# Two transformer blocks with fp32 products: a residual stream turned from features on partitions to tokens on partitions, and half of its products turned with it

## What is computed

```python
# first block
u = rmsnorm(h, g_mix_pre);  proj = u @ w_in            # 2048 -> 10240, then two attentions
mixed = sigmoid(ga) * (oa @ w_br_moba) + sigmoid(gb) * (ob @ w_br_diff)
h = h + rmsnorm(mixed @ w_out, g_mix_post)
ff = square(relu(rmsnorm(h, g_mlp_pre) @ w_up)) @ w_down      # 2048 -> 8192 -> 2048
h = h + rmsnorm(ff, g_mlp_post)
gate = sigmoid(rmsnorm(h, g_ple_pre) @ w_ple_gate)
h = h + rmsnorm((p @ w_ple_proj) * gate, g_ple_post)
# second block
z = rms_norm(x, mix_norm_g) @ w_in;  ...               # mLSTM and forgetting attention
x = x + concat(ha, hb) @ w_out
x = x + (gelu(conv(a)) * g) @ w_down                   # 2048 -> 2 x 5632 -> 2048
x = x + sigmoid(rms_norm(x, ple_norm_g) @ w_ple_gate) * (p @ w_ple_proj)
```

## Time and profile before

| what | value |
|---|---|
| time, median of 3 runs | 2920.16 us (2914.24 to 2925.27) |
| profiled execution: its own time | 2925.14 us |
| its span, first to last instruction | 2923.3 us |
| mean granted clock of TensorE | 0.987 |
| PE busy / weight loads busy | 2832.4 us (97%) / 2451.9 us (84%) |
| DVE / ACT / POOL busy | 1952.9 us (67%) / 1425.3 us (49%) / 180.5 us (6%) |
| matmuls | 15969, of them 2 x 7680 of the large products |
| DMA | 510.29 MB, 175 GB/s; weight transfers of 1024 KB land in 5.2 to 5.7 us |

### The profile page before, as it was taken

The page is one execution under the profiler, slowest core; times in us unless marked ns, Lnnn a source line. Parts: engine busy times, 40 slices in busy tenths (PEclk is TensorE's granted clock), DMA queues, the critical chain, the costliest instruction groups (busy, mean ns, idle before and its releaser), DMA issues.

```text
span 2923.3 us, 43834 instructions
## 1 busy us (share of the span) xinstructions
PE 2832.4 (97%) x15969; PEld 2451.9 (84%) x15969; DVE 1952.9 (67%) x2287; ACT 1425.3 (49%) x1757; POOL 180.5 (6%) x136
## 2 busy tenths in 40 slices
PE   7999999998999999999887999999999999999998
PEld 6888888886888888888776888778888888888877
DVE  6676766667656656566688566766777567667885
ACT  5555554444444444444454545554544444444564
POOL 2000000011000000001212000002100000000210
PEclk9999999999999999999999999999999999999999
DMA  6555546564655556555544355445565555656553
GB/s 216 173 172 171 174 162 192 182 190 126 189 185 183 191 179 194 186 184 185 163 139 122 116 184 161 153 150 187 176 195 190 189 182 191 195 179 201 165 180 130
DMA packets 499727, 510.29 MB, mean 175 GB/s; under 512 B 8586, under 2 KB 496288, under 8 KB 499648
## 3 DMA queue, kind: packets, MB, share of 16 engines
q1 hardware_dynamic: 498576, 508.39, 54.6%
q0 software_dynamic: 1072, 0.83, 0.2%
HBM read 507.09 MB, written 2.10 MB: 174 GB/s over the span
## 4 chain that ended last, share of the span: by engine, by line
PE 90%; DVE 5%; ACT 2%; issue 2%; DMA 0%; POOL 0%; DVEq 0%; SPq 0%; ACTq 0%
PE ps L1620 57%; PE ps L1621 29%; DVE split L981 2%; DVE E L1465 1%; ACT split L539 1%; PE pw L1720 1%; DMA raw<-in_w_in 0%; DVE G L1046 0%; PE pw L1656 0%; ACT X L563 0%; POOL G L431 0%; PE pw L1721 0%; PE pw L1715 0%; DVE X L1012 0%; DVE h L1037 0%
## 5 line engine op out<-in xcount | busy, mean ns | idle before, releaser
L1620 PE MATMUL ps<-X,split 128*128 128x512 f32 x7168 | 2539.0, 399 | 45.9 <-issue 32.0
L1621 PE MATMUL ps<-X,split 128*128 128x256 f32 x7168 | 2011.7, 281 | 0.0
L1620 PEld LDWEIGHTS ps<-X,split 128*128 128x128 f32 x7168 | 1353.6, 189 | 376.1 <-issue 38.3
L981 DVE TENSOR_TENSOR split<-raw,split 128x1024 fp32r<-128x1024 f32 x968 | 1199.0, 1261 | 528.6 <-ACT split L539 521.4
L1621 PEld LDWEIGHTS ps<-X,split 128*128 128x128 f32 x7168 | 1359.1, 190 | 0.8
L539 ACT ACTIVATE split<-raw 128x1024 fp32r<-128x1024 f32 x968 | 1008.6, 1055 | 689.6 <-PE ps L1621 687.0
L545 ACT ACTIVATE cross<-ps 128x512 f32<-128x512 f32 x252 | 150.4, 597 | 411.1 <-PE ps L1621 411.0
L1620 PE MATMUL ps<-split,X 128*128 128x512 f32 x512 | 185.4, 405 | 0.0
L1621 PE MATMUL ps<-split,X 128*128 128x256 f32 x512 | 144.7, 283 | 0.0
L994 DVE TENSOR_TENSOR t<-ps,cross 128x512 f32<-128x512 f32 x90 | 62.2, 691 | 110.4 <-ACT cross L545 110.4
L1620 PEld LDWEIGHTS ps<-split,X 128*128 128x128 f32 x512 | 97.3, 190 | 25.0 <-issue 2.0
(11 more groups left out here) (245 smaller groups left out, 1096.5 us busy)
## 6 DMA issues: line engine op xcount, KB each, us to landing
raw<-in_w_up SPq DMA_DIRECT2D x152, 1024.0 KB, 5.7
raw<-in_w_in SPq DMA_DIRECT2D x136, 1024.0 KB, 5.2
raw<-in_w_down SPq DMA_DIRECT2D x96, 1024.0 KB, 5.4
raw<-in_w_out SPq DMA_DIRECT2D x32, 1024.0 KB, 5.3
raw<-in_w_ple_gate SPq DMA_DIRECT2D x32, 1024.0 KB, 5.4
raw<-in_w_down SPq DMA_DIRECT2D x16, 768.0 KB, 4.5
raw<-in_w_br_moba SPq DMA_DIRECT2D x8, 1024.0 KB, 5.4
raw<-in_w_br_diff SPq DMA_DIRECT2D x8, 1024.0 KB, 5.4
```

The lines of the kernel that those rows point to most:

```text
L981: TT(split[:, k % RING, :, 1, :], raw[:, (k // 2) % RING, HALF * (k % 2):HALF * (k % 2) + HALF, :], split[:, k % RING, :, 0, :], ALU.subtr ...
L1620: MM(ps[:, bank, :], stay_hi, move, start=start, stop=False, skip_group_check=True)
L1621: ins = MM(ps[:, bank, 0:TOK], stay_lo, move[:, 0, :], start=False, stop=stop, skip_group_check=True)
```

## The change

Four things change together.

1. `h` becomes [128, 2, 2048]: tokens on partitions, two token tiles, features along the row. The input lands in it directly and the output is stored from it directly, so L2005 and L776 go, and the input's copy L578.
2. The products whose result is added to `h`, or gated for it (out1, ffn1 down, proj1, gate1, out2, ffn2 and ffn2b down, proj2, gate2), get the form "wide" (`wide_tile`): 128 tokens' activation is stationary and 512 weight columns move, three times (hi by hi, hi by lo, lo by hi) into one region of a bank. No cross half is left, so ACT's copy of it and DVE's add go in these phases; a unit is now 512 features by 256 tokens and lasts 8 halves of 2 tiles. Transfers bring 512 rows by 512 columns.
3. In the form "features", which stays for the other products, the two 512-column matmuls of a tile now come first and the two 256-column ones behind them (before, they alternated).
4. The norms: ACT squares rows with an accumulator (`square`, two of 128x512 for a quarter of the features), DVE sums 4 numbers (`norm_sum`), root and inverse are taken of 128x2 values, and DVE adds `G` times the norm's column to `h` by 2 instructions of 128x512 (`add_normed`). The gains of the post norms are multiplied in when a unit is evacuated, from rows that POOL's transfers bring. Then PE turns each quarter of `h` by 8 transposes (`turn`, L1801), and ACT and DVE make the next operand from PSUM (`gained_hi`, `gained_lo`), in steps of 2 tiles. Where a product needs the norm as a row, PE makes it from a diagonal (`norm_row`). POOL makes no squares any more.

Also, proj1 moves from behind ffn1 to behind out1; the first wide half needs 2 feature tiles of its operand and not 4; and the loops over units of out1, gate1, out2, gate2 and the last downs are written out.

```diff
 PHASES = [
-    ("moba", 4, 8, 4), ("diff", 4, 8, 4), ("branch", 4, 8, 6), ("out1", 4, 4, 2),
-    ("ffn1", 4, 32, 16), ("proj1", 1, 2, 8), ("gate1", 4, 4, 2),
...
+    ("moba", 4, 8, 4, 0), ("diff", 4, 8, 4, 0), ("branch", 4, 8, 6, 0), ("out1", 2, 8, 2, 2), ("proj1", 1, 2, 4, 4),
+    ("ffn1", 4, 32, 12, 4), ("gate1", 2, 8, 2, 2),
...
-    h = sb("h", [P, KT, TOK])
+    h = sb("h", [P, 2, DM])
...
+    wide1, wide2 = ("wide", X1, 0, 8 * (2,)), ("wide", X2, 0, 8 * (2,))
+    OUT1 = GATE = plan([wide1, wide1])
+    OUT2 = DOWN = plan([wide2, wide2])
...
+        def wide(at, g, w, col0, row0=0, rows=2048):
+            for q in range(rows // 512):
+                load(at, g + q, w[bass.ds(row0 + q * 512, 512), bass.ds(col0, WIDE)])
...
+        def square(k, c, tokens):
+            for q in range(2):
+                A(junk[:, :], tokens(q), ACT.Square, accum_out=norm_sq[:, k, q, c:c + 1]).then_inc(squares, 1)
...
-            for k in range(4):
-                kt = 4 * c + k
-                ins = A(X1[:, bass.ds(kt, 1), 0, :], h[:, bass.ds(kt, 1), :], ACT.Copy, scale=vec(gain, kt))
-            ins.then_inc(x1_hi, 1)
+            for pair in range(2):
+                act.wait_ge(x_turned, 8 * norm_of(e) + 2 * c + pair + 1)
+                for k in range(2):
+                    kt = 4 * c + 2 * pair + k
+                    ins = A(X1[:, kt, 0, :], pw[:, 2 * (c % 2) + pair, k * TOK:k * TOK + TOK], ACT.Copy, scale=vec(gain, kt))
+                ins.then_inc(x1_hi, 1)
...
+        def add_normed(k, c, src):
+            for q in range(2):
+                ins = STT(h[:, q, columns(c)], src(q), norm_col[:, k, q:q + 1], h[:, q, columns(c)], ALU.mult, ALU.add)
+            ins.then_inc(h_ready, 1)
...
                 for j in range(2):
-                    bank, js = 2 * s + j, slice(j * P, j * P + P)
...
-                    MM(ps[:, bank, :], stay_hi, move, start=start, stop=False, skip_group_check=True)
-                    ins = MM(ps[:, bank, 0:TOK], stay_lo, move[:, 0, :], start=False, stop=stop, skip_group_check=True)
+                    MM(ps[:, 2 * s + j, :], stay[:, 0, j * P:j * P + P], move, start=start, stop=False, skip_group_check=True)
+                for j in range(2):
+                    ins = MM(ps[:, 2 * s + j, 0:TOK], stay[:, 1, j * P:j * P + P], move[:, 0, :], start=False, stop=stop, skip_group_check=True)
...
+        def wide_tile(s, x, w, start, stop):
+            for q in range(2):
+                dst = ps[:, 2 * s + q, :].rearrange("p (a c) -> p a c", a=2)
+                x_hi, x_lo = (x[:, part, q * P:q * P + P] for part in range(2))
+                MM(dst, x_hi, w[:, :, 0, :], start=start, stop=False, skip_group_check=True)
+                MM(dst, x_hi, w[:, :, 1, :], start=False, stop=False, skip_group_check=True)
+                ins = MM(dst, x_lo, w[:, :, 0, :], start=False, stop=stop, skip_group_check=True)
...
+        def turn(e, c):
+            if c >= 2:
+                pe.wait_ge(x1_ready, 8 * e + 2 * c - 2)
+            for pair in range(2):
+                for k in range(2):
+                    kt = 4 * c + 2 * pair + k
+                    for q in range(2):
+                        ins = T(pw[:, 2 * (c % 2) + pair, k * TOK + q * P:k * TOK + q * P + P], h[:, q, kt * P:kt * P + P], ident)
+                ins.then_inc(x_turned, 1)
```

More of the change, by code:

```diff
@@ L1274, in embed, with out1, after @@
             TT(operand[:, :, 1, :], pw[:, 2, :].rearrange("p (a t) -> p a t", a=2), operand[:, :, 0, :], ALU.subtract).then_inc(p_ready, 1)
+        def out1(i):
+            s = At("out1", i, 8, 2)
+            def after(m):
+                if i == 0 and m == 2:
+                    embed(0, X2[:, 12:14])
+                if m % 8 == 7:
+                    n = 2 * i + m // 8
+                    row = gain_row(n)
+                    if n == 3:
+                        norm_sum(1)
+                    else:
+                        dve.wait_ge(squares, 8 + 2 * n + 2)
+                    TT(G_tok[:, :, columns(n)], wide_sums(s, m, m // 8), row, ALU.mult).then_inc(evac_done, 1)
+            each_half(s, OUT1, after)
+        out1(0)
+        out1(1)
+        norm_inverse(1)
+        dve.wait_ge(evac_done, U0["out1"] + 4)
+        s = At("proj1")
+        add_normed(1, 0, of_G(0))
+        add_normed(1, 1, of_G(1))
+        lo(s, 0)
+        add_normed(1, 2, of_G(2))
+        gained_lo(2, 0, "g_mlp_pre")
+        lo(s, 1)
+        add_normed(1, 3, of_G(3))
+        lo(s, 2)
+        gained_lo(2, 1, "g_mlp_pre")
+        lo(s, 3)
+        gained_lo(2, 2, "g_mlp_pre")
         def ffn1(b):
@@ L1528, in _, with add_h, out2, after @@
-        out2 = add_h("out2", TILES_OUT2, TWO, operand=(5, "ffn_norm_g_2"))
+        def add_h(at, m, u, n):
+            cs = columns(n)
+            dve.wait_ge(evac_done, at.unit(u))
+            TT(h[:, :, cs], h[:, :, cs], wide_sums(at, m, u), ALU.add).then_inc(evac_done, 1)
+        def out2(i):
+            s = At("out2", i, 8, 2)
+            def after(m):
+                if i == 0 and m == 2:
+                    finish_fox(1)
+                if m % 8 == 4 and (i or m > 7):
+                    gained_lo(5, 2 * i + m // 8 - 1, "ffn_norm_g_2")
+                if m % 8 == 7:
+                    add_h(s, m, m // 8, 2 * i + m // 8)
+            each_half(s, OUT2, after)
@@ L1805, in embed, with out1, before, proj_unit @@
             ins.then_inc(p_turned, 1)
+        def out1(i):
+            s = At("out1", i, 8, 2)
+            def before(m):
+                if i == 0 and m == 2:
+                    embed(0)
+            each_half(s, OUT1, x1_is(1), before)
+        out1(0)
+        out1(1)
+        def proj_unit(at, u, op, tile):
+            g = u // 2
+            unit_start(at, u)
+            if u % 2 == 0:
+                pe.wait_ge(lo_done, at.halves(2 * g) + 2)
+            first = blocks(at, 2 * g, u, "wide", op, u % 2, (tile,), True, False)
+            last = blocks(at, 2 * g + 1, u, "wide", op, u % 2, (tile + 1,), False, True)
+            if u % 2 == 0:
+                last.then_inc(pair_used, 1)
+            else:
+                first.then_inc(half_used, 1)
+                last.then_inc(half_used, 1)
@@ new lines, in _, with start_up, hidden @@
+        out2(0)
+        out2(1)
+        def ffn2(name, b, pairs, k0):
+            outer = dict(outer_turn=b * 12, outer_units=b * 20, outer_cross=b * 16) if name == "ffn2" else {}
+            first = name == "ffn2" and isinstance(b, int) and b == 0
+            def start_up(m):
+                if m == 1:
+                    pe.wait_ge(evac_done, U0["out2"] + 4)
+                    turn(5, 3)
+                if m == 4:
+                    norm_row(3, 0)
+            def hidden(m, u, upto):
```

987 lines of the change are left out of this document (520 added, 467 removed).

## The result

| | before | changed |
|---|---|---|
| median, same chip | 2922.7 us (2914.2 to 2938.5) | 2836.9 us (2834.6 to 2837.7) |
| ratio | | 0.9709, 95% interval 0.9681 to 0.9737 |
| profiled execution, and its span | 2925.1 us, 2923.3 us | 2836.1 us, 2834.3 us |

The kernel is faster by 85.8 us in the medians and by 89.0 us between the two profiled spans. The forecast was a gain of 41.5. The time fell in the predicted range, but about half of the gain has a cause to which the forecast gave nothing.

A forecast was written before the change was run, and what follows sets the result against it. PE, busy 97% of the span, was taken as the bound. Seams gain 42.1 us, extra transposes lose 4.6, the start gains 4: 41.5 in all, so 2883.6 us for a profile and 2879 for the median; range 2828 to 2908.

The forecast's parts named there:

- the pace goes by columns: Dense products: a matmul costs only its columns, so 1.5 wide matmuls cost what a 512 plus 256 pair costs; gain 0.
- the new order: Features form, 512, 512, 256, 256: same columns and loads as the alternating order, so costed at 0.
- rival 1: Dense products: the overhead is per matmul, a wide one takes 0.229 us, 22 us more gained, 2857; chance 0.15.
- the two paces: Pairs took 0.354 us in ffn1, 0.3475 in ffn2; which one a phase falls into may move 25 us either way.
- load rule: Skill's rule: a weight load takes its columns divided by 1.2 GHz, so wide matmuls would hide loads; rejected from the trace.
- The seams: Excess over dense work between phases and at the tail: 88.2 us before, 46.1 after, a gain of 42.1.
- 4.6 lost to transposes: Out2, ffn2 and ffn2b: added transposes and a norm row, less one `sum_acc`, cost 2.1 plus 2.5 us.
- the cover: Out1 to ffn1: two units of proj1, 5.6 us, stand ahead of the first transpose and hide the norm's 5.3 us chain.
- The start: First window, 51 us: the input's copy on ACT and POOL's summing go; gain 4 us.
- Rival 2: Dense products: wide matmuls run at full pace, 0.215 us each, 80 us more gained, 2799; chance 0.06.
- rival 3: Seams stay long: PE waits 1.9 us for each of four quarters at three seams, 23 us lost, 2902; chance 0.08.
- rival 4: Wide matmuls read two runs 2 KB apart and slow down; at 0.249 us each plus 63 us, 2942; chance 0.11.

The follow-up runs named there:

- Run 3: The changed kernel with each 512-column matmul of the wide form issued as two of 256, same columns and stationary blocks: 2887.4 us, a single run.
- Run 2: The changed kernel with the features products back in the old order 512, 256, 512, 256: 2848.5 us, against the changed kernel's 2836.9.
- run 1: The kernel before with only the new order, both 512-column matmuls ahead of the two 256-column ones: 2906.7 us against 2918.0, ratio 0.9967.
- run 5: The changed kernel with the operands of the wide form read as bfloat16, same number and columns of matmuls: 2827.9 us, a single run.
- Run 6: The changed kernel with proj1's products cut to one matmul per bank and tile, 7.3 us of PE work taken out: 2834.4 us, 2.5 less.
- run 7: The changed kernel with one more 128x256 reciprocal on VectorE in each of the three norms that add to the residual stream: 2840.4 us, 3.6 more.
- run 10: The control: the changed kernel itself, unchanged, measured again on another chip: 2836.9 us, ratio 0.9713 to before.

## Why the prediction was right and where it was wrong

- **The direction and the range held, the size didn't.** 41.5 us were forecast and 85.8 measured. The term that failed is in the part on the wide matmul: "the pace goes by columns ... this edit gives 0", and the next one, the new order "I cost it at 0". That the range held is partly luck: for the forecast alone the prediction gave 2850 to 2908, and 2836.9 lies in the part below, which it kept for its first rival. Its own sign, "I am wrong if the time moves inside the dense stretches, and not at the seams", came half true: the time moved in both.
- **The wide edit.** In place of 2816 pairs at 0.351 (988 us) there are 4224 matmuls at 0.2268 (958): 30 us, not 0. Run 3 shows the mechanism, cost per matmul: at 346.7 ns, columns and fixed cost alone, the pairs would have been 976 us, so 18 of the 30 come from fewer matmuls. The other 12 are what the old pairs took beyond that, which belongs to their order. The cost per matmul is rival 1, given 0.15; it had 0.229 for a wide matmul and 22 us.
- **The order.** 4864 pairs at 0.351 became 2432 quads at 0.697: 12 us, not 0. Run 2, with the same pairs, measures 11.7, and run 1, with 7680, 11.4 (2 to 17). The prediction saw the two paces, took them for a lottery of the stage and put 25 us to either side (counted on 7680 pairs; only 4864 keep the form, which is 16). Only the old order has the two paces; what picks between them under it is not shown.
- **Why the reading misled.** I fitted a + b per column to the start distances inside a mixed stream: 0.237 and 0.117, a ratio of two. In a pure stream they are 0.2268 and 0.1203. In the mixed one the 512-column step reads 7 ns too long and the 256-column step 3 ns too short, and just this makes them look proportional. Only the sum of a repeating group can be trusted there, and one sum can't give two unknowns. The trace of before did hold a warning: at 1.2 GHz a pair took 0.64 us, exactly its 768 columns, and at 2.4 GHz 0.347 at best, not 0.320. Something beyond the columns costs 27 ns a pair there, as rival 1 said; whether it goes by matmul or by column only a second width shows.
- **Weight loads.** The rejection of the Trainium skill's load rule (TensorE: Matmul & The Clock Gate, "LDWEIGHTS (loading the stationary operand)") as the limit holds: beside the earlier trace rows, run 5 halved the loads to 96 ns and moved the pace by 1.4 ns. The loads' mean stayed at 188 ns in the changed kernel.
- **The seams** of the table gained 43.1 us, forecast 42.1. With the start's 2.4 that leaves 0.5 of the 46, where the prediction had 4.6 lost to transposes in out2, ffn2 and ffn2b; this loss does not show in the remainder, and I did not trace why. The head of the seam to gate1 was 9.48 (forecast 9.3), the tail 6.6 (6.5), proj2 1.4 (2.0). out1 to ffn1 was 9.8 instead of 7.8; of this 2.3 are the wait for the norm's row, which I had at 0.4 in all. Run 6 supports the cover, and run 7 the chain and that the cover has no slack.
- **The start.** 4 us were forecast; the first 51 us have 28.5 of excess before and 26.1 now, so 2.4 came. A new wait of 1.5 us for the norm's row stands in this stretch (2.7 in run 10).
- **Rival 2** (0.215) is refuted by 0.2268, **rival 3** (seams stay long, 2902) by the table above, **rival 4** (the operand in two runs) by run 3.

## What to carry to other kernels

Price a dense matmul stream as columns plus a fixed cost per matmul, and get the two numbers from streams of one width each, never from single distances in a mixed stream. The same group at both clocks tells whether there is a cost beyond the columns, not what it goes by. Fewer, wider matmuls for the same columns then pay by a sum that can be written down, and where widths must mix, try the order: equal widths next to each other were 11 to 12 us faster here. In a seam ask which engine's chain ends last before spending on another: 1.75 us more on VectorE cost 1.6 in each seam, while a clock kept at double speed through two seams gave 0.8 in all.

## What the runs showed that I had not expected

- The fixed cost is 13.3 ns per product matmul at 2.4 GHz and is not to be seen at 1.2 GHz: there a wide matmul starts 0.42 to 0.43 us after the one before it (behind the seam from ffn1 to gate1), and 512 / 1.2 GHz is 426.7 ns.
- The same four matmuls in the order 512, 256, 512, 256 take 0.693 or 0.707 us, and 0.697 in the order 512, 512, 256, 256 in all the long dense stretches (ffn1, ffn2); in attention, among small products, it is 0.702 and more. The faster of the old paces is thus a little better than the new one, and I have no explanation for what picks the slower.
- While GpSimd summed on 128x1024 early in the kernel before, VectorE's split of the same size took about twice its length. GpSimd's and VectorE's rows there:

```profile
27.90 1.22 DVE L981 TENSOR_TENSOR split<-raw,split 128x1024 fp32r<-128x1024 f32 x1
...
29.20 9.05 POOL L431 TENSOR_TENSOR G<-G 128x1024 f32<-128x1024 f32 x3 [17.50 <-ACT G L596]
...
30.10 2.60 DVE L981 TENSOR_TENSOR split<-raw,split 128x1024 fp32r<-128x1024 f32 x1 [0.98 <-ACT split L539]
```

  With most of GpSimd's work gone, the mean of this operation fell from 1261 to 1223 ns over 960 of them. Nearly all of that is beside TensorE; in the stretch shown it waited 1.0 us in all for two of these splits.
